# Two token tiles of a strip through its weights together, quarter by quarter

## The reference, cut to what matters

```
y = concatenate([o_gdn, c], -1) @ w_out        # stage "mix": (1024 x 1024) @ (1024 x 1024)
h = h + rmsnorm(y, g[1])                       # residual and norm of the mixer
q = rmsnorm(h, g[2]) @ w_q                     # stage "xq", attention follows

y = o @ w_o                                    # stage "xo": (1024 x 1024) @ (1024 x 1024)
h = h + rmsnorm(y, g[3])
u = rmsnorm(h, g[4]) @ w_up                    # stage "ffn", first product
```

## Time and profile before

| | |
|---|---|
| median of 3 runs | 2670.04 us (2668.05 to 2671.69) |
| the profiled execution's own time | 2670.99 us |
| its span | 2669.2 us |
| mean granted TensorE clock | 0.992 of full speed |
| TensorE busy | 2591.1 us, 97% of the span |
| GpSimd busy | 1131.9 us, 42% |
| VectorE busy | 1659.6 us, 62% |
| ScalarE busy | 844.0 us, 32% |

### The profile page before, as it was taken

The page is one execution under the profiler, slowest core; times in us unless marked ns, Lnnn a source line. Parts: engine busy times, 40 slices in busy tenths (PEclk is TensorE's granted clock), DMA queues, the critical chain, the costliest instruction groups (busy, mean ns, idle before and its releaser), DMA issues.

```text
span 2669.2 us, 33144 instructions
## 1 busy us (share of the span) xinstructions
PE 2591.1 (97%) x13218; PEld 2174.4 (81%) x13218; DVE 1659.6 (62%) x2194; ACT 844.0 (32%) x1332; POOL 1131.9 (42%) x651
## 2 busy tenths in 40 slices
PE   6999899989999999999999999999999999999998
PEld 5788788877788777888888887888888888888887
DVE  4879978766512587666674558804555556476566
ACT  4011233334223433333332436212222222343342
POOL 2433100046632548777754444673223322242364
PEclk9999999999999999999999999999999999999999
DMA  4122333235312412222245553573333342466682
GB/s 153 56 94 97 99 124 127 95 104 206 112 62 79 158 58 86 79 87 79 87 149 191 169 178 121 186 258 106 134 111 111 130 147 94 159 251 211 223 315 111
DMA packets 147381, 360.25 MB, mean 135 GB/s; under 512 B 15173, under 2 KB 51229, under 8 KB 147100
## 3 DMA queue, kind: packets, MB, share of 16 engines
q1 hardware_dynamic: 65072, 177.81, 19.9%
q10 hardware_dynamic: 82156, 180.33, 18.9%
HBM read 268.90 MB, written 89.19 MB: 134 GB/s over the span
## 4 chain that ended last, share of the span: by engine, by line
PE 89%; DVE 4%; POOL 2%; ACT 2%; issue 1%; DMA 1%; ACTq 0%; POOLq 0%; DVEq 0%
PE pp L296 32%; PE pp L2213 13%; PE pp L494 11%; PE pp L2266 9%; PE pp L278 9%; PE pp L2953 2%; PE pp L1272 2%; POOL w_lo L3653 1%; PE pp L1944 1%; PE pp L1983 1%; POOL w_hi L3651 1%; DMA w_raw<-in_weights 1%; PE pp L1558 1%; PE pp L1597 1%; PE pp L444 1%
## 5 line engine op out<-in xcount | busy, mean ns | idle before, releaser
L3651 POOL CAST w_hi<-w_raw 128x1024 fp32r<-128x1024 f32 x184 | 222.2, 1207 | 990.3 <-PE pp L296 659.5
L296 PE MATMUL pp<-w_hi,act_hi 128*128 128x512 f32 x1344 | 535.9, 399 | 12.7 <-POOL w_lo L3653 9.9
L296 PE MATMUL pp<-w_lo,act_hi 128*128 128x512 f32 x1344 | 524.5, 390 | 0.0
L296 PE MATMUL pp<-w_hi,act_lo 128*128 128x512 f32 x1344 | 524.5, 390 | 0.0
L3653 POOL TENSOR_TENSOR w_lo<-w_raw,w_hi 128x1024 fp32r<-128x1024 f32 x184 | 468.9, 2549 | 14.7
L296 PEld LDWEIGHTS pp<-w_hi,act_hi 128*128 128x128 f32 x1344 | 253.0, 188 | 67.9 <-POOL w_lo L3653 10.8
L296 PEld LDWEIGHTS pp<-w_hi,act_lo 128*128 128x128 f32 x1344 | 252.6, 188 | 53.5
L296 PEld LDWEIGHTS pp<-w_lo,act_hi 128*128 128x128 f32 x1344 | 253.2, 188 | 48.3
L494 PE MATMUL pp<-act_hi,w_hi 128*128 128x512 f32 x480 | 192.7, 402 | 10.6 <-DVE act_lo L849 6.5
L2184 POOL TENSOR_TENSOR w_lo<-w_raw,w_hi 128x1024 fp32r<-128x1024 f32 x52 | 132.5, 2550 | 164.7 <-ACT w_hi L2178 164.6
L494 PE MATMUL pp<-act_lo,w_hi 128*128 128x512 f32 x480 | 190.5, 397 | 0.0
(11 more groups left out here) (468 smaller groups left out, 5282.9 us busy)
## 6 DMA issues: line engine op xcount, KB each, us to landing
w_raw<-in_weights SPq DMA_DIRECT2D x314, 512.0 KB, 3.5
z_s<-hg_st ACTq DMA_DIRECT2D x52, 512.0 KB, 4.1
hid_s<-ffn_cb ACTq DMA_DIRECT2D x22, 512.0 KB, 2.6
ffn_graw<-hid_s ACTq DMA_DIRECT2D x44, 256.0 KB, 3.1
hg_qkb<-hT_s SPq DMA_DIRECT2D x16, 512.0 KB, 8.1
qkvT_s<-mixin_o ACTq DMA_DIRECT2D x12, 512.0 KB, 2.8
gdn_qkv<-qkvT_s ACTq DMA_DIRECT2D x8, 768.0 KB, 6.4
front_x<-in_x ACTq DMA_DIRECT2D x8, 512.0 KB, 5.0
```

The lines of the kernel that those rows point to most:

```text
L296: last = pe.matmul(dst, a[:, k, t * P:(t + 1) * P], columns(w, j, k, 0, n), start=(k == 0 and a is high and w is w_hi), stop=(k == NK - 1 ...
L3651: pool.tensor_copy(hi, raw).then_inc(w_split, 1)
```

## The change

Units i = 2 and i = 3 of a strip are no longer made one after the other. `last_two` makes them together: for each quarter of the weights six matmuls of tile 2 into its PSUM bank, then six of tile 3 into the next one, so that TensorE changes bank every six matmuls. A quarter is released after tile 3's six. Both `made` counts are given in the last quarter. Nothing changes in units 0 and 1 of a strip, in the units that are made early, or in what the other engines are told to do.

```
+            def last_two(self, pe, k):
+
+                half, s, i = k // (N_OUT * self.HT), k // self.HT % N_OUT, k % self.HT
+                j = self.first + half * N_OUT + s
+                for n in range(2):
+                    prior(pe, self.kept, "kept", k + n - 4)
+                for q in range(HALVES[j]):
+                    ks = range(NK // HALVES[j] * q, NK // HALVES[j] * (q + 1))
+                    for n in range(2):
+                        last = product_rows(pe, j, half * self.HT + i + n, self.dst(k + n), final=(n == 1), ks=ks)
+                        if q == HALVES[j] - 1:
+                            self.made.done(last, "made")
...
-                    self.unit(pe, k)
+                    if k % self.HT == self.HT - 2:
+                        self.last_two(pe, k)
+                    elif k % self.HT < self.HT - 2:
+                        self.unit(pe, k)
```

## The result

The changed kernel took 2673.91 us (median of 15 runs, 2671.49 to 2677.45), the kernel before in the same measurement 2669.17 (15 runs, 2665.94 to 2671.69). The ratio is 1.002, with a 95% interval of 1.0012 to 1.0028: slower by about 4.7 us, near the edge of what the prediction called no change (0.2%, 5.3 us). The prediction said 2672.2, with a range of 2667.5 to 2675.5, and +2.2 us as the difference. The profiled execution of the changed kernel took 2673.41 us with a span of 2671.6, against 2670.99 and 2669.2 before.

What follows compares the result with a forecast made beforehand. TensorE, 89% of the chain that ended last, was taken to bound the kernel. Terms of -3.9 (unit 8), +2.2 (end of mix) and +3.9 (xo) gave +2.2 us: 2673.2 profiled, 2672.2 as median, range 2667.5 to 2675.5.

Steps and rivals of the forecast that it cites:

- Part 1: Unit 8 in mix and xo: earlier release of slots removes both TensorE waits for split weights, -3.9 us (2 x 1.96).
- Part 2: Seven pairs of tiles, three in mix and four in xo: changing PSUM bank every six matmuls costs TensorE 0.
- Part 3: Ends of mix and xo: unit 14 finishes late, so TensorE's next stage starts 4.1 us later in mix, 2.15 in xo.
- Part 4: Behind the longer waits for keep(15) in mix and xo: the granted clock falls, 1.7 us each, lower bound 0.
- Part 5: Turn 6 in mix: its 1.88 us wait and slow clock go, leaving mix's end +2.2 us; xo keeps +3.9.
- the likeliest case: Whole kernel: the summed terms hold, 2672.2 us, with its own range of 2670.2 to 2674.2; chance 58%.
- the full range: Whole kernel: 2667.5 to 2675.5 us, leaving out the gain alone, most of the 10% case and the clock.
- No stretch in mix: End of mix: GpSimd's earlier start misses scale 4 and 5; sum +0.2 us, 2670.2; chance 20%.
- the end of mix isn't swallowed: Turn 6 in mix waits again, so the 4.1 and 1.7 are paid in full; +5.8 us, 2675.8; chance 10%.
- the clock fall in the pairs: Seven pairs, 336 matmuls, 76 us: at half the clock +76 us, 2746; chance 1%.
- Only the gain: Waits in unit 8 go and keep(15) isn't late: -3.9 us, 2666.1; chance 6%.
- The waits in unit 8 stay: Unit 8: waits remain because GpSimd's two quarters take over 11.9 us; +2 to +6 us; chance 5%.

Runs made afterwards that it cites:

- run 9: The change, with the first four loads of x in mix bringing 128 of 1024 columns each (part of the residual left out): 2672.06 us against 2669.18 before.
- run 1: The change with the pair form in every strip but the last of each stage: 2665.43 us against 2668.38 for the kernel before.
- run 3: The change, with ScalarE copying unit 15 out of PSUM right behind unit 14: 2666.76 us against 2668.38 for the kernel before.
- run 4: The change, but units 14 and 15 release no quarter until the next stage's first matmul: 2669.84 us against 2668.38 for the kernel before.
- run 5: Run 1's form, with the second to fourth loads of x in mix issued later: 2668.33 us against 2668.44 for the kernel before.
- run 6: The kernel before, with only the second to fourth loads of x in mix issued later: 2670.87 us against 2668.44 without it.
- run 10: Run 1's form, in mix gains and x of tile 0 loaded behind first(1), other x behind keep(6), first(2), keep(7): 2671.42 us against 2669.18 before.

## Why the prediction was right or wrong

**Part 1, the two waits: right in xo, wrong in mix. This is the step that failed.** "The first quarter is released ... 619.8, when GpSimd has just finished the work before." The release came when it said, in both stages; xo won 1.98 us for 1.96. But I had checked that GpSimd was free and that the slot was, and not that the raw quarter was there. It took 7.8 us to land, beside 3 MB of gains and x that ScalarE's queue issues just behind the start of unit 5. The old wait for a slot had hidden this second one behind it (4.50 us for the slot, 4.38 for the data); in the kernel before the data had landed 0.2 us before the cast. The term -3.9 should have been -2.1; run 9 shows the missing part come back when the transfers go.

**Part 2, the changes of bank: right.** Between the start of unit 1 and unit 14 in xo, with three pairs in it, the changed trace is 1.98 us shorter, all of it the wait. Run 1, with five pairs, has the lowest ratio of all kernels here. The rule that the prediction cited from the Trainium skill (TensorE: Matmul & The Clock Gate, "A second HAM failure mode: psum-queue depth-cycling", small gaps between groups of matmuls in turning banks let the clock fall) does not bear on this kernel: in the changed trace the matmuls of a pair start 0.227 us apart across the changes of bank, with no gap between the groups, and the granted clock is 1.00 in all seven pairs.

**Part 3, unit 14's lateness: right, in mechanism and size.** 4.35 and 2.12 us for 4.1 and 2.15; runs 3 and 4 take it apart as forecast, 2.15 from ScalarE's list and 2.2 from GpSimd's earlier start.

**Part 4, the clock: right on average, too sure of itself.** Behind the new waits it fell as forecast in the changed profile, and cost 2.28 and 1.62 us for 1.7 each. But it isn't a rule that a wait of this length brings it down; the last section has the counts.

**Part 5, what swallows it: half right.** Turn 6's wait went, as the chain said, and its slow clock with it. But that slow clock, 1.7 us, need not be there: in four other profiles with the same wait at turn 6 (runs 1, 5, 6 and 10) the clock stayed up. By these counts most executions of the kernel before did not have it, and had nothing to give back; the profiles are too few to say how many. For an execution without it the sum by the measured pieces is -0.1 + 4.35 + 2.28 - 2.03 in mix and +1.76 in xo, +6.2; with the slow clock of the profile given back +4.5. The measured +4.7 (3.2 to 7.5 by the interval) lies with both. How the 15 runs divide between them no profile of one execution can tell, and this stays open.

**The total.** The measured 2673.91 lies 1.7 us above the forecast of 2672.2, and inside the range of the likeliest case by 0.3. That flatters the working. As a difference to the kernel before, +4.7 was measured for +2.2, 2.5 us off; 0.9 of it doesn't show in the time, because the kernel before measured 2669.17 now, where the forecast had started from 2670.04. By the whole 2.5 it would have missed the range of the likeliest case and not the full range. In the profile the two stretches are 2.4 us longer than forecast: 1.8 for the wait in unit 8, 0.6 for the deeper fall of the clock and 0.2 for the later first product in mix, less some small pieces. The direction and most of the size rest on parts 3 and 4, and these were right; that the figure came so close with part 1 half wrong is luck.

**The rivals.** "No stretch in mix" and "the end of mix isn't swallowed" did not happen: VectorE was stretched, turn 6 did not wait. Nor did the clock fall in the pairs. "Only the gain" is what runs 1 and 3 come near (-3.0 and -1.6 us for -3.9), with the wait in unit 8 of mix still there. "The waits in unit 8 stay" came true for mix, by a cause that I hadn't named: data, not GpSimd's speed.

## What to carry to other kernels

When an edit frees a buffer earlier, ask of the engine that is to fill it for all that it waits for: the trace names only the wait that ended last, and another can have ended just ahead of it (here by some 0.2 us). Work that is interleaved to finish together frees inputs early and finishes outputs late; where the list of the engine that takes the outputs off puts other work between them, the second output's reader pays. Here it paid to leave the interleaving out of the last round before another stage (run 1), or to take the two outputs off back to back (run 3). What an edit gives back by ending a slow clock in one profile should be counted by how often it falls there in several.

## What the runs showed of the hardware

Twelve profiles (before, after, ten experiments) have waits of nearly equal length at the same place of the program, with TensorE at work at full pace ahead of them. How often the granted clock fell to 0.50 to 0.68 in the 4 us behind:

```
wait of TensorE       where                         fell
1.88 to 1.89 us       turn 6 in mix                 1 of 5
2.01 us               behind turn 7 in xo           4 of 12
2.79 to 2.84 us       first product behind mix, xo  5 of 6
5.04 us               first product behind mix      4 of 4
```

The same wait in the same place does both. Behind the waits of 1.0 to 1.7 us in these two stretches it never fell. Two waits stand alone: behind 2.21 us in unit 8 (run 6) it stayed up, behind 2.48 us at turn 0 (run 10) it fell to 0.65. From 1.9 us up to 2.8 the length of the wait alone doesn't decide it, as I had expected it to, and no run here shows what does. Behind the first product one fall cost 1.5 to 2.5 us of TensorE time (first product to turn 4 in nine places of five profiles, 7.05 to 8.05 us for 5.58).

And a load of 512 KB that lands in 3.4 us alone (that of `w_raw` issued at 607.90 us in the kernel before) took 7.8 us with the six of the gains and x under way (the third quarter in the changed kernel), all together at 419 GB/s from 616 to 620 us.
